# Two-block decoder kernel: 128 tokens of the expert layer gathered instead of 96, 384 dense columns instead of 416, weight splits and roundings moved between engines

## The chip, the cores and the metric

The kernel runs on one core of one Trainium2 chip. The metric is the device time in microseconds (us). Before the change three runs gave 3052.07, 3065.22 and 3062.26 us, median 3062.26. The execution that the hardware profiler took lasted 3056.66 us and has a span of 3054.9 us.

## The reference

512 tokens of width 1024 go through a first block (convolution and latent attention in parallel, then an expert layer called PEER) and a second block of two layers (short convolution, sparse attention, each with a gated feed-forward layer). The change is in the expert layer alone:

```
q = (xb @ wq).reshape(C, PEER_HEADS, 2, PEER_DK_HALF)
s = jnp.einsum('chpd,hpnd->chpn', q, keys)          # 8 heads, 2 halves, 128 keys
sv, si = lax.top_k(s, 16)
cand = sv[:, :, 0, :, None] + sv[:, :, 1, None, :]
top_s, sel = lax.top_k(cand.reshape(C, PEER_HEADS, 256), 16)
eidx = ...                                            # one of 16384 experts, 8 x 16 a token
g = jax.nn.softmax(top_s, axis=-1)
act = gelu(einsum('chkd,cd->chk', u_tab[eidx], xb))
out = einsum('chk,chkd->cd', g * act, v_tab[eidx])
```

Each token chooses 128 of the 16384 experts, each a row of 1024 numbers in the table `peer_u` and one in `peer_v`.

## The kernel before, in words

Activations lie transposed, features on partitions. Every product of fp32 numbers is done as three products of rounded high and low parts (`product`, L305 to L309). Weight tiles (128 x 1024, 512 KB) run through `Feed`, a ring with three slots: SyncE (SP) loads a tile when the tile three before it is split (L253), ScalarE (ACT) rounds it to the high part when TensorE (PE) is done with the tile three before it (L262), and the low part is subtracted (L272, the "split") by VectorE (DVE) in the expert layer and by GpSimd (POOL) elsewhere.

The expert layer (`peer`) treats most tokens densely. All 16384 experts are computed for the first 416 tokens: a **U phase** of 128 tiles, of 24 products each, gives activations that ACT passes through gelu (L1627) and SP stores to DRAM (L1422); then a **V phase** of 128 tiles multiplies them, weighted with gates, into the eight PSUM banks. The gates are zero but for the chosen experts. They are built in the U phase from one-hot vectors: `gate_block` (L1528) makes eight tokens' gates with 16 small products, ACT copies them (L1608), SP stores them. In the V phase SP loads them again, eight tiles' gates at once (`load_gates`, L1409, 1664 KB), along with each tile's activations (L1415).

The last 96 tokens are gathered: POOL fetches expert rows by indirect DMA (L1463) into four buffers; VectorE multiplies each with the token's row and adds up (`first`, L1707, a dot) for the first table, and adds it with its weight (`second_of`, L1861) for the second. 64 tokens lie on two partitions each and 32 on four, so 96 steps of 128 rows do for each table; a spread of small DMAs (SP, L1423 to L1430) puts ids and token rows there, and products with `fold` matrices add the copies together at the end (L1570).

Which experts a token chooses is found by VectorE in four **routes**, one for each 128 tokens (L1721 to L1838): top 16 of 128 scores by `max`, `max_index` and `match_replace`, the sums, the top 16 again, and the decoding of places by comparisons. The order of the routes is 3, 0, 1, 2, so that the gathered tokens come first. All orders are written out by hand: `START`, `score_tile`, `turn_tile` and `block_tile` say at which U tile TensorE computes scores, turns the results of a route (`turn`, which waits for VectorE) and does which gate block. A route lasts 15 tiles, and within it VectorE calls `weights()` at 15 places, each of which splits the next tile. In the gate-block stretches VectorE does for each tile a split, the one-hot vectors (`hots`), and one dot (`early`); after the last route two dots a tile until 76 are done. The other 20 dots and all 96 steps of the second table are done in the V phase, at most one a tile. There VectorE does for tile n, in this order: gates times activations (L1880), the gather step, the weight split, the rounding of the weighted activations (L401) and their low part (L404). TensorE waits for the last of these.

Engines execute their instructions in order, and a wait holds all behind it.

Of the kernel before, what the change touches and what calls it, by code (L numbers as in the profile page):

```python
# [35 lines left out]
F32 = mybir.dt.float32  # L36
# [7 lines left out]
P = 128  # L44
# [179 lines left out]
class Feed:  # L224
# [50 lines left out]

    def take(self, pe, n):
        pe.wait_ge(self.split, n + 1)
        return self.hi[:, n % self.SLOTS, :], self.lo[:, n % self.SLOTS, :]


class Part:
# [12 lines left out]
    def split_to(self, eng, m):  # L294
        self.feed.split_to(eng, self.first + m)

# [915 lines left out]
GROUPS = ((64, 448), (32, 416))  # L1212
STEPS = sum(n for n, first in GROUPS)
DTOK = SEQ - STEPS
ROWS = 4
ROUTE = (3, 0, 1, 2)
Q_WEIGHTS = 15
EARLY = 76


def peer(kit, io):
# [4 lines left out]
    with Stage(kit, "peer") as st:  # L1226
# [38 lines left out]
        groups, small = [], 44032  # L1265
        for g, (n, first) in enumerate(GROUPS):
            s0 = sum(m for m, _ in GROUPS[:g])
            groups.append(dict(n=n, first=first, s0=s0, rep=P // n,
                               mine=at(f"chosen_here{g}", small, [P, 2, n], U32),
                               fold=at(f"fold{g}", small + 8 * n, [P, n])))  # L1270
            small += 12 * n
        dots = at("dots", small, [P, STEPS])
        share = at("shares", small + 4 * STEPS, [P, STEPS])
        assert small + 8 * STEPS <= 46080 and 2 * DTOK * QUAD * 4 <= 26624
        group_of = [g for g in groups for _ in range(g["n"])]
# [7 lines left out]
        rows = nc.alloc_sbuf_tensor_at("peer_token_rows", [P, D], F32, offset=G_at)  # L1283
        chosen = nc.alloc_sbuf_tensor_at("peer_chosen", [P, 2, PH * TOPK], U32, offset=G_at + 4 * D)
        for g, x in enumerate(groups):
            x["acc"] = nc.alloc_sbuf_tensor_at(f"peer_gather_sum{g}", [P, D], F32, offset=shared + g * D * 4)
# [8 lines left out]
        groups[0]["row"] = nc.alloc_sbuf_tensor_at("peer_row_here0", [P, D], F32, offset=io["mixT_at"] + 12288)  # L1295
        for g, x in enumerate(groups[1:]):
            x["row"] = st.sb(f"row_here{g + 1}", [P, D])
# [34 lines left out]
        spread = st.sem("tokens_spread")  # L1332
# [33 lines left out]
        TURN = Q_WEIGHTS + 1  # L1366
        blocks, START, of_route = [], [], []
        for r, j in enumerate(ROUTE):
            START.append(Q_WEIGHTS * r + len(blocks))
            mine = list(range(j * P, min((j + 1) * P, DTOK), HB))  # L1370
            of_route.append(range(len(blocks), len(blocks) + len(mine)))
            blocks += mine
# [9 lines left out]
        scored_first = sum(c <= TURN and half == 0 for c, (r, half) in score_tile.items())  # L1382
        n_spread = 32 * sum(x["rep"] for x in groups)
# [7 lines left out]
        def second_step(n):  # L1391
            return n - SHARES - 1 if 0 <= n - SHARES - 1 < STEPS else None

        with nc.Block() as block:

            @block.sync
            def _(sp):
# [19 lines left out]
                for c in range(NK + 1):  # L1417
# [5 lines left out]
                    if c == TURN + 3:  # L1423
                        sp.wait_ge(experts_known, 2)
                        sp.wait_ge(rows_copied, 1)
                        for x in groups:
                            n, t0 = x["n"], x["first"] - (SEQ - P)
                            for e in range(x["rep"]):
                                sp.dma_start(x["mine"][e * n:(e + 1) * n, :, :],
# [1540 lines left out]
```

## Time and profile before

| | |
|---|---|
| median of 3 runs | 3062.26 us |
| profiled execution | 3056.66 us, span 3054.9 us |
| PE busy | 2918.0 us, 96% of the span |
| PE weight loads (PEld) | 2591.1 us, 85% |
| DVE busy | 1802.1 us, 59% |
| ACT busy | 996.8 us, 33% |
| POOL busy | 999.0 us, 33% |
| U phase | 376.8 to 1068.2 us |
| V phase | 1068.2 to 1652.0 us |
| mean granted TensorE clock | 0.956 |

Busy times of PE and PEld overlap. A granted clock of 1 is 2.4 GHz; the lower level is 1.2 GHz. Times of an event are counted from the start of the span.

### The profile page before, as it was taken

Reading aid. Unit: us, or ns where it says so; the run is one execution under the profiler, and the core shown is the slowest. Engines: PE = TensorE matmul, PEld = TensorE weight load, DVE = VectorE, ACT = ScalarE, POOL = GpSimd, SP = SyncE. Lnnn points to the kernel's source line nnn. Section 1 sums busy time; section 2 is a strip of 40 time slices with the busy share of each in tenths; the row PEclk is TensorE's granted clock in tenths of the full one; section 3 lists DMA queues with packets and bytes.
Section 4 is the critical chain, followed back from the end, with each engine's and each line's share of the span. In section 5 each row is a group of like instructions: output and inputs, shape, how many; then the busy total and the mean of one; then the engine's idle time right before and its main releaser. Section 6 shows DMA issues by size and latency. Waiting matters only on the chain. (4 is left out here: it accounts for less than half of the span.)

```text
span 3054.9 us, 39382 instructions
## 1 busy us (share of the span) xinstructions
PE 2918.0 (96%) x15042; PEld 2591.1 (85%) x15042; DVE 1802.1 (59%) x3227; ACT 996.8 (33%) x1582; POOL 999.0 (33%) x611
## 2 busy tenths in 40 slices
PE   8887999999999799999999999999999899999998
PEld 7554799999999799999998787888788898778886
DVE  6785777888887677887884843331143455333311
ACT  4345233443434222222223223222223456332212
POOL 3201500111112432433332544444432344454442
PEclk9767999999999899999999999999999789999999
DMA  3101256786959988999983232233331000223332
GB/s 130 34 1 42 95 145 206 225 277 200 296 179 308 385 294 304 329 324 329 331 305 113 90 104 83 97 97 102 98 130 31 4 1 15 76 83 97 97 103 70
DMA packets 195745, 475.83 MB, mean 156 GB/s; under 512 B 17205, under 2 KB 104117, under 8 KB 193253
## 3 DMA queue, kind: packets, MB, share of 16 engines
q1 hardware_dynamic: 167764, 370.54, 37.0%
q0 software_dynamic: 27648, 100.68, 9.5%
q8 instruction: 120, 1.97, 0.3%
q10 hardware_dynamic: 144, 2.10, 0.2%
q14 instruction: 69, 0.56, 0.0%
HBM read 415.47 MB, written 56.62 MB: 155 GB/s over the span
## 5 line engine op out<-in xcount | busy, mean ns | idle before, releaser
L262 ACT ACTIVATE w_hi<-w 128x1024 fp32r<-128x1024 f32 (+2 forms) x485 | 506.6, 1046 | 1236.3 <-DVE ffn_gates L2119 324.4
L272 POOL TENSOR_TENSOR w_lo<-w,w_hi 128x1024 fp32r<-128x1024 f32 (+2 forms) x229 | 542.4, 2379 | 693.6 <-ACT w_hi L262 693.6
L272 DVE TENSOR_TENSOR w_lo<-w,w_hi 128x1024 fp32r<-128x1024 f32 x256 | 313.5, 1225 | 190.7 <-ACT w_hi L262 158.5
L307 PE MATMUL peer_psum<-xn_hi,w_hi 128*128 128x416 f32 x1024 | 369.0, 360 | 16.2 <-ACT peer_act_out L1627 16.2
L308 PE MATMUL peer_psum<-xn_lo,w_hi 128*128 128x416 f32 x1024 | 363.2, 355 | 0.0
L309 PE MATMUL peer_psum<-xn_hi,w_lo 128*128 128x416 f32 x1024 | 362.7, 354 | 0.0
L307 PE MATMUL peer_psum<-peer_w_hi,w_hi 128*128 128x416 f32 x1024 | 359.8, 351 | 2.1 <-DVE peer_w_lo L404 1.4
L308 PE MATMUL peer_psum<-peer_w_lo,w_hi 128*128 128x416 f32 x1024 | 358.9, 350 | 0.0
L309 PE MATMUL peer_psum<-peer_w_hi,w_lo 128*128 128x416 f32 x1024 | 358.9, 350 | 0.0
L1463 POOL DMA_INDIRECT peer_gathered<-in_peer_u,peer_chosen_here x96 | 141.5, 1474 | 623.0 <-DVEq L1710 496.0
L307 PE MATMUL ffn_psum<-ffn_hn_hi,w_hi 128*128 128x512 f32 x704 | 275.8, 392 | 10.4 <-DVE ffn_hn_lo L617 6.6
L308 PE MATMUL ffn_psum<-ffn_hn_lo,w_hi 128*128 128x512 f32 x704 | 275.2, 391 | 0.0
L309 PE MATMUL ffn_psum<-ffn_hn_hi,w_lo 128*128 128x512 f32 x704 | 275.2, 391 | 0.0
L1463 POOL DMA_INDIRECT peer_gathered<-in_peer_v,peer_chosen_here x96 | 168.0, 1750 | 281.9 <-DVEq L1865 269.9
L307 PEld LDWEIGHTS peer_psum<-xn_hi,w_hi 128*128 128x128 f32 x1024 | 195.8, 191 | 19.6 <-issue 17.6
L308 PEld LDWEIGHTS peer_psum<-xn_lo,w_hi 128*128 128x128 f32 x1024 | 195.8, 191 | 1.3
L309 PEld LDWEIGHTS peer_psum<-xn_hi,w_lo 128*128 128x128 f32 x1024 | 195.2, 191 | 1.4
L307 PEld LDWEIGHTS peer_psum<-peer_w_hi,w_hi 128*128 128x128 f32 x1024 | 192.4, 188 | 4.2 <-issue 2.1
L308 PEld LDWEIGHTS peer_psum<-peer_w_lo,w_hi 128*128 128x128 f32 x1024 | 192.4, 188 | 1.1
L309 PEld LDWEIGHTS peer_psum<-peer_w_hi,w_lo 128*128 128x128 f32 x1024 | 192.4, 188 | 1.0
L1627 ACT ACTIVATE peer_act_out<-peer_psum 128x416 f32<-128x416 f32 x128 | 66.3, 518 | 340.1 <-PE peer_psum L309 280.3
L307 PEld LDWEIGHTS ffn_psum<-ffn_hn_hi,w_hi 128*128 128x128 f32 x704 | 133.0, 189 | 41.5 <-issue 7.4
(417 smaller groups left out, 5724.5 us busy)
## 6 DMA issues: line engine op xcount, KB each, us to landing
w<-in_peer_uT SPq DMA_DIRECT2D x128, 512.0 KB
w<-in_peer_v SPq DMA_DIRECT2D x128, 512.0 KB
w<-in_f_w_gu SPq DMA_DIRECT2D x88, 512.0 KB
peer_act<-peer_act_out SPq DMA_DIRECT2D x128, 208.0 KB
peer_gate<-peer_gates_out SPq DMA_DIRECT2D x26, 1024.0 KB, 8.1
peer_gates<-peer_gate SPq DMA_DIRECT2D x16, 1664.0 KB, 9.6
peer_act_in<-peer_act SPq DMA_DIRECT2D x128, 208.0 KB
w<-in_f_w_down SPq DMA_DIRECT2D x32, 512.0 KB
```

What stands on the lines that cost most here:

```text
L262: act.activation(self.hi[:, x, 0:c], self.buf[:, x, 0:c], ACT.Copy).then_inc(self.rounded, 1)
L272: eng.tensor_tensor(self.lo[:, x, 0:c], self.buf[:, x, 0:c], self.hi[:, x, 0:c].bitcast(F32), ALU.subtract).then_inc(self.split, 1)
L307: pe.matmul(out, w[0], x[0], start=start, stop=False)
L308: pe.matmul(out, w[0], x[1], start=False, stop=False)
L309: return pe.matmul(out, w[1], x[0], start=False, stop=stop)
L1463: pool.indirect_dma_start(G[:, s % ROWS, :], None, table, bass.IndirectOffsetOnAxis(here[:, 0, at0:at0 + 1], 0))\
L1627: act.activation(Ao[:, c % AS, 0:DTOK], ps[:, c % 2, 0:DTOK], ACT.Gelu).then_inc(gelued, 1)
```

## The change

The gathered tokens are the first 128, one on each partition: 128 steps for each table, no spread, no fold matrices, and the token rows stay where ACT wrote them. The dense columns are tokens 128 to 511, 384 of them; gate blocks are 48. Routes run in the order 0 to 3, with 13, 16, 16 and 16 tiles. In a route POOL splits the weight tiles and, from route 1 on, fetches one row set behind each split; VectorE calls `beside` at the places where it split before, which does one dot (every fourth time two), none in route 0. After the routes one dot a tile is done until 112. In the V phase ACT rounds the weighted activations, behind its rounding of the next weight tile; VectorE does 16 dots and then spreads the 128 steps of the second table over 107 tiles. The first load of gates goes out eight tiles before the end of the U phase, the second in the V phase.

```diff
+    def split_one(self, eng, n):
+        c, x = self.tiles[n].shape[1], n % self.SLOTS
+        eng.wait_ge(self.split, n)
+        eng.wait_ge(self.rounded, n + 1)
+        eng.tensor_tensor(self.lo[:, x, 0:c], self.buf[:, x, 0:c], self.hi[:, x, 0:c].bitcast(F32),
+                          ALU.subtract).then_inc(self.split, 1)
...
-GROUPS = ((64, 448), (32, 416))
-STEPS = sum(n for n, first in GROUPS)
-DTOK = SEQ - STEPS
+GT = 128
+STEPS = PH * TOPK
+DTOK = SEQ - GT
 ROWS = 4
-ROUTE = (3, 0, 1, 2)
-Q_WEIGHTS = 15
-EARLY = 76
+Q_WEIGHTS = (13, 16, 16, 16)
+EARLY = 112
+PACE = 99
...
-            turn_tile[START[r] + TURN] = r
+            turn_tile[START[r] + Q_WEIGHTS[r] + 1] = r
             for i, b in enumerate(of_route[r]):
-                block_tile[START[r] + TURN + 1 + i] = b
+                block_tile[START[r] + Q_WEIGHTS[r] + 3 + i] = b
...
+        def dot_beside(b):
+            return b not in of_route[0] and b % PACE != PACE - 1
...
-        def second_step(n):
-            return n - SHARES - 1 if 0 <= n - SHARES - 1 < STEPS else None
+        def second_steps(n):
+            return [s for s in range(STEPS) if SHARES + 1 + s * (NK - 2 - SHARES) // STEPS == n]
...
-                    if c == TURN + 3:
-                        sp.wait_ge(experts_known, 2)
-                        sp.wait_ge(rows_copied, 1)
-                        for x in groups:
...
-                    if c == NK - 6:
+                    if c == NK - 8:
                         for i in range(2):
                             sp.wait_ge(g_stored[i], 16 * len(range(i, n_slices, 2)))
-                        for q in range(2):
-                            load_gates(q)
+                        load_gates(0)
+                    if c == NK - 6:
                         for n in range(AS):
                             sp.wait_ge(a_stored[n], 16)
                             load_act(n)
...
                     load_act(n)
+                    if n == AS + 1:
+                        load_gates(1)
...
-                pool.wait_ge(spread, n_spread)
-                for s in range(2 * STEPS):
+                fetched_to = 0
+                for r in range(ST):
+                    for n in range(Q_WEIGHTS[r]):
+                        lin.ring.split_one(pool, U0 + START[r] + n + 2)
+                        if r == 1 and n == 0:
+                            pool.wait_ge(experts_known, 2)
+                            for s in range(ROWS):
+                                fetch(s, t["peer_u"])
+                            fetched_to = ROWS
+                        if r:
+                            fetch(fetched_to, t["peer_u"])
+                            fetched_to += 1
+                    for b in of_route[r]:
+                        if dot_beside(b):
+                            fetch(fetched_to, t["peer_u"])
+                            fetched_to += 1
+                for s in range(fetched_to, 2 * STEPS):
                     fetch(s, t["peer_u"] if s < STEPS else t["peer_v"])
...
-                                     xn.pair(slice(None), k, slice(0, DTOK)), k == 0, k == DT - 1)
+                                     xn.pair(slice(None), k, slice(GT, SEQ)), k == 0, k == DT - 1)
...
-                            for x in groups:
-                                mm = pe.matmul(ps[:, d, x["first"]:x["first"] + x["n"]], x["acc"][:, p], x["fold"][:, :],
-                                               start=True, stop=True)
+                            mm = pe.matmul(ps[:, d, 0:GT], acc[0:GT, p], kit.ident[0:GT, 0:GT], start=True, stop=True)
...
-                lin.ring.round_to(act, V0 + SHARES)
-                act.wait_ge(dotted, 1)
-                act.activation(dots[:, :], dots[:, :], ACT.Gelu).then_inc(dots_gelued, 1)
+                for n in range(NK):
+                    lin.ring.round_to(act, V0 + n + 2)
+                    if n == SHARES - 1:
+                        act.wait_ge(dotted, 1)
+                        act.activation(dots[0:GT, :], dots[0:GT, :], ACT.Gelu).then_inc(dots_gelued, 1)
+                    if n >= WS:
+                        lin.ring.done_by(act, V0 + n - WS + 1)
+                    act.wait_ge(weighed, n + 1)
+                    act.activation(Ws.hi[:, n % WS, 0:DTOK], Wf[:, n % 2, 0:DTOK], ACT.Copy).then_inc(w_hi, 1)
...
                 def weights():
 
                     ahead[0] += 1
-                    lin.ring.split_to(dve, U0 + min(ahead[0] + 2, NK))
+                    lin.ring.split_one(dve, U0 + ahead[0] + 1)
...
+                def beside(r):
+
+                    placed[r] += 1
+                    for _ in range((2 if placed[r] % 4 == 0 else 1) if r else 0):
+                        early()
...
-                    if n >= WS:
-                        lin.ring.done_by(dve, V0 + n - WS + 1)
                     lin.ring.split_to(dve, V0 + n + 1)
-                    dve.wait_ge(weighed, n + 1)
-                    Ws.write_hi(dve, (slice(None), n % WS, slice(0, DTOK)), x).then_inc(w_hi, 1)
                     dve.wait_ge(w_hi, n + 1)
                     Ws.write_lo(dve, (slice(None), n % WS, slice(0, DTOK)), x).then_inc(w_lo, 1)
```

## Rows read from the trace of the kernel before

**Rows 1.** Stretches, all engines: length, busy PE, PEld, DVE, ACT, POOL, clock, DMA share, GB/s

```profile
376.80:1068.20 691.40, 665.26 (x4076) 645.70 (x4076) 552.25 (x1394) 262.65 (x390) 115.60 (x82) 0.98 0.77 247
1068.20:1652.00 583.80, 582.12 (x3104) 578.22 (x3104) 469.09 (x646) 136.04 (x130) 193.87 (x110) 1.00 0.85 302
```

**Rows 2.** Waits in the U phase: who waited for whom, us, times, longest

```profile
PE peer_psum L307 <- ACT peer_act_out L1627: 16.2, 3, 11.6
```

**Rows 3.** Timeline: start us, us, what; PE at 264 columns, ACT at 416, POOL at 512

```profile
97.83 0.28 PE L309 MATMUL front_psum<-xn_hi,w_lo 128*128 128x264 f32 x1
...
100.38 0.29 PE L309 MATMUL front_psum<-xn_hi,w_lo 128*128 128x264 f32 x1
...
1404.74 1.06 ACT L262 ACTIVATE w_hi<-w 128x1024 fp32r<-128x1024 f32 x1 [3.46 <-PE peer_psum L309]
...
1440.90 1.06 ACT L262 ACTIVATE w_hi<-w 128x1024 fp32r<-128x1024 f32 x1 [3.46 <-PE peer_psum L309]
...
1819.50 2.40 POOL L272 TENSOR_TENSOR w_lo<-w,w_hi 128x1024 fp32r<-128x1024 f32 x1 [3.04 <-ACT w_hi L262]
```

**Rows 4.** Timeline of weight loads in the U phase, one gate block

```profile
475.63 0.90 PEld L1528 LDWEIGHTS peer_psum<-peer_first_hot,peer_second_hot 128*128 128x128 f16 x16 [0.18 <-issue]
```

**Rows 5.** Timeline of DVE in the V phase, one tile

```profile
1401.35 0.58 DVE L1880 SCALAR_TENSOR_TENSOR peer_w<-peer_gates,peer_act_in 128x416 f32<-128x416 f32 x1
1401.85 1.28 DVE L1861 SCALAR_TENSOR_TENSOR peer_gather_sum<-peer_gathered,peer_shares,peer_gather_sum 128x1024 f32<-128x1024 f32 x1
1403.34 1.23 DVE L272 TENSOR_TENSOR w_lo<-w,w_hi 128x1024 fp32r<-128x1024 f32 x1 [0.21 <-DVE peer_gather_sum L1861]
1404.49 0.37 DVE L401 CAST peer_w_hi<-peer_w 128x416 fp32r<-128x416 f32 x1
1404.89 0.59 DVE L404 TENSOR_TENSOR peer_w_lo<-peer_w,peer_w_hi 128x416 fp32r<-128x416 f32 x1
```

**Rows 6.** Timeline of SP's loads and ACT's roundings in the V phase, two pairs

```profile
1088.28 0.43 SPq L253 DMA_DIRECT2D w<-in_peer_v  x1
...
1093.47 1.06 ACT L262 ACTIVATE w_hi<-w 128x1024 fp32r<-128x1024 f32 x1 [3.46 <-DMA w<-in_peer_v]
...
1402.80 1.51 SPq L253 DMA_DIRECT2D w<-in_peer_v  x1
...
1414.02 1.06 ACT L262 ACTIVATE w_hi<-w 128x1024 fp32r<-128x1024 f32 x1 [8.22 <-DMA w<-in_peer_v]
```

**Rows 7.** Stretch in the U phase: length, PE busy, clock, DMA share, GB/s

```profile
540.00:580.00 40.00, 38.07 (x228) 0.96 0.57 177
```

**Rows 8.** Stretches with gate stores (PE alone) and in the V phase (columns as rows 1)

```profile
740.00:780.00 40.00, 39.86 (x300) 1.00 0.93 300
...
1300.00:1600.00 300.00, 300.00 (x1595) 298.20 (x1594) 248.03 (x327) 70.93 (x67) 111.36 (x63) 1.00 0.90 324
```

**Rows 9.** Timeline of ACT at the end of the U phase

```profile
1059.76 0.52 ACT L1627 ACTIVATE peer_act_out<-peer_psum 128x416 f32<-128x416 f32 x1 [18.22 <-DMA peer_act<-peer_act_out]
```

**Rows 10.** One route: DVE busy in it, and its splits alone

```profile
481.90:554.70 72.80, 59.71 (x234) 1.00 0.72 224
...
481.90:554.70 72.80, 18.37 (x15) 1.00 0.72 224
```

**Rows 11.** Timeline of DVE in the U phase, a dot and what follows

```profile
643.09 1.22 DVE L1707 SCALAR_TENSOR_TENSOR peer_gathered<-peer_gathered,peer_row_here 128x1024 f32<-128x1024 f32 x1
...
644.46 1.23 DVE L272 TENSOR_TENSOR w_lo<-w,w_hi 128x1024 fp32r<-128x1024 f32 x1
```

**Rows 12.** Timeline of POOL and DVE in the next stage; L2014 by itself

```profile
1791.33 2.59 POOL L272 TENSOR_TENSOR w_lo<-w,w_hi 128x1024 fp32r<-128x1024 f32 x1 [0.75 <-ACT w_hi L262]
...
1791.70 2.77 DVE L2014 SCALAR_TENSOR_TENSOR hT<-hT,gains,short_gf_rs 128x512 f32<-128x512 f32 x1
...
L2014 DVE SCALAR_TENSOR_TENSOR hT<-hT,gains,short_gf_rs x8: 751/1760/2770, 1702.2 to 1791.7; 128x512 f32<-128x512 f32 x8
```

**Rows 13.** Groups in the U phase: busy us, mean ns, idle before

```profile
L1463 POOL DMA_INDIRECT peer_gathered<-in_peer_u,peer_chosen_here x82 | 115.6, 1410 | 578.8 <-DVEq L1710 451.8 <-DMA peer_row_here<-peer_token_rows 124.9 <-issue 2.1
```

More of the change, by code:

```diff
@@ L1263, in peer @@
         A = at("act_in", 46080, [P, AS, SEQ])
[L1265 to L1275, printed above, removed]
+        mine = at("chosen", 44032, [P, 2, STEPS], U32)
+        dots = at("dots", 45056, [P, STEPS])
+        share = at("shares", 45568, [P, STEPS])
+        assert 2 * DTOK * QUAD * 4 <= 26624
         shared = nc.sbuf_base
@@ L1282, in peer @@
         G = nc.alloc_sbuf_tensor_at("peer_gathered", [P, ROWS, D], F32, offset=G_at)
[L1283 to L1286, printed above, removed]
+        acc = nc.alloc_sbuf_tensor_at("peer_gather_sum", [P, D], F32, offset=shared)
         an_bufs = (at("an_sq", 4096, [P, 2, SEQ]), at("an_rs", 8192, [P, SEQ]), io["attn_sum"])
@@ L1365, in peer @@
         PER = HB // 4
-        TURN = Q_WEIGHTS + 1
         blocks, START, of_route = [], [], []
[L1368 to L1372, printed above, removed]
+        for j in range(ST):
+            START.append(sum(Q_WEIGHTS[:j]) + len(blocks))
+            here = list(range(max(j * P, GT), (j + 1) * P, HB))
+            of_route.append(range(len(blocks), len(blocks) + len(here)))
+            blocks += here
         n_blocks, per_slice = len(blocks), QB // HB
@@ L1726, in _ @@
                         if i == 7:
-                            weights()
+                            beside(r)
                     own.wait()
-                    weights()
+                    beside(r)
                     for i in range(NS):
@@ L1733, in _ @@
                         if i % 6 == 5:
-                            weights()
+                            beside(r)
                     own.wait()
@@ L1739, in _ @@
                         if i == 7:
-                            weights()
+                            beside(r)
                     own.wait()
-                    weights()
+                    beside(r)
                     for i in range(NS):
@@ L1762, in _ @@
                     own.wait()
-                    weights()
+                    beside(r)
                     for h in range(PH):
@@ L1767, in _ @@
                     own.wait()
-                    weights()
+                    beside(r)
                     for h in range(PH):
@@ L1773, in _ @@
                         own.step(dve.max_index(sel[:, h, 8:16], tops[:, h, 8:16], left[:, h, :]))
[L1774 removed]
+                    beside(r)
                     own.step(dve.tensor_copy(tot[:, :], tops[:, :, 0]))
@@ L1797, in _ @@
                                                abf[:, 2:4, :].rearrange("p i (h k) -> p i h k", h=PH), ALU.add))
-                    weights()
+                    beside(r)
                     for i in range(2):
@@ L1803, in _ @@
                     own.wait()
-                    weights()
+                    beside(r)
                     for i in range(2):
@@ L1812, in _ @@
                     own.link(dve.tensor_tensor(three[:, 0:2, :], eq[:, :, 0, :], eq[:, :, 1, :], ALU.add))
-                    weights()
+                    beside(r)
                     dve.wait_ge(exped, r + 1)
@@ L1868, in _ @@
                     weights()
-                    for _ in range(2):
-                        early()
+                    early()
                 assert dotted_to[0] == EARLY
+                if EARLY == STEPS:
+                    own.wait()
+                    dve.nop().then_inc(dotted, 1)
                 for n in range(NK):
```

88 lines of the change are left out of this document (36 added, 52 removed).

## The prediction

> **What bounds the kernel now.** I read the table of stretches first: the expert part is two stretches. In the first (the U phase, 376.8 to 1068.2 us) TensorE multiplies the 128 weight tiles of `peer_uT`; in the second (the V phase, 1068.2 to 1652.0) those of `peer_v`. TensorE is busy 665.3 of 691.4 us and 582.1 of 583.8 [rows 1]. All other stretches run code that the change leaves alone, so the sum is made over these two. Next the waits of TensorE: in the U phase the largest is 16.2 us, behind ScalarE's copy of the results [rows 2]; in the V phase there is next to none. So a saving on TensorE counts in full unless something else becomes late, and a new lateness counts in full too.
>
> Then I ask whether TensorE is paced by its weight loads, since the loads' busy share reaches 99% in the V phase. The starts of consecutive products say no. With 264 columns, 21 products take 2.55 us, 121 ns each, with the same 128-column loads. With 416, eight tiles of 24 products take 36.16 us (from one tensor-released rounding to the one eight tiles later), 188.3 ns each. With 512 a tile lasts 2.40 + 3.04 us, 226.7 ns each [rows 3]. The load records overlap; the columns set the pace. Between the first two widths a column costs 0.44 ns, between the last two 0.40.
>
> **Part 1, 416 to 384 columns.** 32 columns fewer at 0.40 to 0.44 ns are 12.8 to 14.1 ns; I take 14, so a product takes 174.3 ns and a tile 4.18 us where it took 4.52. The 2 x 3072 products of the two phases would save 43 us each, 86 us together, if their operands came in time. The gate blocks fall from 52 to 48; one holds TensorE for about 0.9 us [rows 4]: 4 us saved. The eight pairs of fold products at the end become eight products: about 2 us.
>
> **Part 2, the V phase: a wait that moves.** Before, VectorE did all for tile n by itself: gate times activation (start to start 0.50 us), one gather step (1.49), weight split (1.15), rounding (0.40), low part (0.59): 4.1 us [rows 5]. After it drops the rounding, does 128 gather steps over 107 tiles (1.20 x 1.49 = 1.78 us) and comes to 4.0 us, still under 4.18. The rounding (some 0.5 us, as ScalarE's copy of 416 columns, 0.52 [rows 9]) goes to ScalarE, which has room: its weight rounding is 1.06 us. But ScalarE issues its work in order: it rounds weight tile n+1 and only then the activations of tile n. So tile n cannot start on TensorE until the weights of n+1 have landed, and 1.06 + 0.5 + VectorE's low part and handovers, 2.3 us in all, have passed. Before, tile n+1's weights were needed one tile later.
>
> How late do they land? The load issued at 1402.80, right behind a load of gates, is rounded at 1414.02 (loads and roundings paired by counting), 11.2 us later, where TensorE would have allowed it at 1404.74 + 4.52 = 1409.26; a load with nothing in front takes 1093.47 - 1088.28 = 5.2 us [rows 6]. TensorE did not feel it, since it took that tile at 1418.3. (The same recurs every 36 us, at each load of gates.) After: the load of tile m goes out when VectorE has weighed tile m-2, and VectorE is now itself tied to ScalarE, so it goes out some 3.6 us after TensorE starts tile m-4 (2.3 for the low part of m-3, 0.5 to weigh, 0.8 for SP's issues in front of it). It has to have landed 2.3 us before TensorE starts tile m-1. That leaves 3 x 4.18 - 2.3 - 3.6 = 6.6 us. An ordinary load (5.2 us) fits. One behind the gates (1536 KB where it was 1664, so about 10.3 us) is 3.7 us late, and TensorE stands. The load two tiles later goes out late in turn, behind a queue not yet drained: nothing to 2.4 us more, I take 1.2. A stop of about 2 us also lowers the clock: the stretch with such a stop shows a granted clock of 0.96 over 40 us [rows 7], 3.2 us at the lower of two levels, so 1.5 us more. A period of eight tiles is then 33.4 + 3.7 + 1.2 + 1.5 = 39.8 us, where it was 36.2. There are 14 such periods and 16 tiles without: 14 x 39.8 + 16 x 4.18 = 624 us. At the start of V, VectorE can no longer run ahead of TensorE (ScalarE must first finish the U phase), and tile 3 waits for activations that are fetched only after the last of them is stored: 6 us, bounds 1 and 12. Sum 630 less 2 for the fold: **+44 us** against 583.8. Bounds: 540 us (no stop, -44), and 655 (+71).
>
> The bytes are the check. Per tile 0.52 MB of weights, 0.20 of activations, 0.20 of gates and 1.2 x 0.52 gathered are 1.55 MB; at 39.8 us for eight that is 311 GB/s. The DMA engines gave 324 at a share of 0.90 in the V phase and 300 at 0.93 while gates are stored [rows 8]. At 4.18 us a tile they would have to give 370, so the full column gain is unlikely there even without the moved wait.
>
> **Part 3, the U phase.** While gates are stored each tile moves 0.52 + 0.20 + 0.52 + 0.52 = 1.77 MB; at 300 / 0.93 = 322 GB/s that takes 5.5 us, about what such a tile took before (4.52 + 0.96). So I count no column gain in the 48 block tiles, and 80 x 24 x 14 ns = 27 us in the others. (Bounds 27 and 43.)
>
> The end of U: two loads of gates were issued together six tiles before the end, and two gather steps ran per tile; a result copy then waited 18.2 us for its buffer [rows 9], most of the 16.2 us of [rows 2]. Now one load of gates goes out earlier and one gather step runs per tile: I take 14 us saved with the clock, bounds 5 and 19.
>
> The routes. One route costs VectorE 59.7 us of which 18.4 are splits: 41.3, say 42 with handovers [rows 10]. Splits go to POOL; in routes 1 to 3 come 18 dot products (first-table steps) at 1.37 us each [rows 11]: 66.7 us. The time that TensorE gives: from when VectorE is through with the last gate block to the next turn are one block tile and fifteen plain ones, with VectorE's lead some 70 us; for route 1, 67. That would just fit. But POOL's split and a VectorE instruction with two SBUF inputs get in each other's way: at 1791.33 POOL starts a split of 2.59 us, VectorE starts at 1791.70 an instruction that takes 0.75 us at its shortest, and it takes 2.77, to just after the split's end [rows 12]. In a route POOL splits 2.4 of every 4.18 us, so a dot meets a split in 57 of 100 cases and waits half of it: 0.69 us, 18 times 12.4, and some 2 for the other two-input instructions. That makes 81 us: TensorE stands at the turn 14 us in route 1 and 11 in route 2. In route 3 the dots are just as far as the fetches, so each waits for a split (ends 3.9 us after the tile starts), an indirect fetch (1.4 us [rows 13]), its landing and itself. As many bytes took a plain load 5.2 us from issue to use; for the landing behind the 1.4 I take 3, and the dot is 1.4: dot 15 ends 9.8 us into its tile, 11 us of routing and two dots are left, and the turn is due 8.4 us after that tile's start: 13 us late. Together 38 us and three drops of the clock at 1.5: **43 us**. Bounds: 5 (waits fall into the slack) and 65: in route 1, POOL's fetch waits for the dot and its next split for the fetch, 1.4 + 2.4 + 1.4 = 5.2 us a round where TensorE wants 4.18.
>
> The Trainium skill, "SBUF — State Buffer", section "SBUF: two separate sides", has the rule behind it: the port pair that VectorE and GpSimd share is an exclusive lock, and the later one waits for the whole instruction. The trace agrees (2.77 us for 0.75). By the rule a part of the splits' relief comes back as waiting, 43 us in the sum; without it the routes would cost only route 3's 13.
>
> The spread of chosen experts and rows over groups (12 small DMAs behind SP's wait) goes: 1 us at most, off the path.
>
> U phase: -27 - 4 - 14 + 43 = -2 us. **Sum:** 3056.7 - 2 + 44 = 3099 us for a profiled execution; the median of the three runs shown (3062.3) lies 5.6 above the profiled one, so 3104.
>
> **Rivals.** A: the column gain arrives. V runs at 4.18 us a tile with few stops (550 us) and the routes fit (10 us late): U -27 - 4 - 14 + 10 = -35, V -34, so 2993. For it: VectorE has slack in both phases, and a share of 0.90 leaves the DMA engines a tenth. Against: the 11.2 us behind every load of gates, 14 of them.
> B: DMA alone sets V. The 188 MB that V moves at 321 GB/s take 586 us, the moved wait costs nothing beyond that, routes 25 us late: U -20, V +2, so 3044. For it: shares near 0.9 already. Against: before, loads could land five to six us late unseen.
> C: the round of dot, fetch and split that hands the lock back and forth (5.2 against 4.18 us) holds in all three routes: 48 rounds at 1 us, with clock drops 65 us, and V at its upper bound 655: 3062 + 20 + 71, 3153. It decides from the point where POOL's split of a tile ends after TensorE asks for it.
> D: the change moves work but VectorE gains nothing, since every split taken off it is waited for in the lock. It is the upper half of C's U phase, in C's chance.
>
> **Chances.** Forecast 0.48 (own range 3070 to 3145), A 0.22, B 0.2, C 0.1. A measurement tells a change from none at about 0.5%, 15 us: 3047 to 3078. Faster: A and half of B and a little, 0.33. Same: the rest of B and the forecast's low end, 0.15. Slower 0.52. Range 2990 to 3155.
>
> **What would show it.** Right: TensorE's waits in V appear once per eight tiles, released by `peer_w_lo` and preceded by ScalarE's rounding waiting for the DMA of `peer_v`; the granted clock in V falls under 1; products start 174 ns apart; dots in routes last over 2 us; the turn of each route is waited for; the wait at the end of U is gone. Wrong: ScalarE's roundings in V are released by TensorE only (then A), products stay 188 ns apart (no column gain), or VectorE's dots keep 1.22 us beside POOL's splits.

## The result and the profile after

| | before | after |
|---|---|---|
| median | 3059.5 us (4 runs, 3052.1 to 3065.2) | 3149.7 us (4 runs, 3144.5 to 3152.2) |
| profiled execution | 3056.7 us | 3152.0 us |
| U phase, first product to first product of V | 687.9 us | 718.4 us |
| V phase, first to last product | 583.2 us | 645.0 us |

The change made the kernel slower by 3.0% (ratio 1.030, 95% interval 1.027 to 1.033), 90 us where the forecast had 42. The direction holds, and so does the wide range (2990 to 3155); the forecast's own range, 3070 to 3145, was missed by 5 us, and the size is more than twice the forecast. Between the profiled executions 95.3 us were lost: 30.5 in U, 61.8 in V, 3.0 elsewhere.

The stretches below are cut at the first product of a phase, so that kernels compare: before, then after. Columns: stretch, length, busy PE, granted clock, DMA share, GB/s.

```profile
380.50:1068.40 687.90, 661.59 (x4061) 0.98 0.77 247
1068.40:1651.60 583.20, 581.72 (x3100) 1.00 0.85 302
```

```profile
383.60:1102.00 718.40, 625.64 (x3998) 0.94 0.78 253
1102.00:1747.00 645.00, 569.64 (x3088) 0.93 0.83 292
```

TensorE is busy for 48 us less and idle for 140 us more, and the granted clock is lower. The waits of TensorE after, in U (four rows) and in V (the last), as [rows 2]:

```profile
PE peer_psum L1514 <- DVE peer_three L1835: 37.5, 3, 15.0
PE peer_psum L319 <- ACT peer_act_out L1631: 23.8, 4, 13.6
PE peer_psum L1534 <- ACT peer_gates_out L1612: 22.7, 10, 5.5
PE peer_psum L319 <- POOL w_lo L280: 7.0, 7, 2.2
...
PE peer_psum L319 <- DVE peer_w_lo L416: 76.7, 19, 6.8
```

**V.** The waits come once per eight tiles. Two of TensorE's starts after such a wait, 40.72 us apart:

```profile
1449.17 0.66 PE L319 MATMUL peer_psum<-peer_w_hi,w_hi 128*128 128x384 f32 x1 [3.91 <-DVE peer_w_lo L416]
...
1489.89 0.66 PE L319 MATMUL peer_psum<-peer_w_hi,w_hi 128*128 128x384 f32 x1 [4.58 <-DVE peer_w_lo L416]
```

ScalarE shows why. Between stops it rounds a weight tile every 4.16 us, released by TensorE: that is the new tile, 24 products of 173 ns. Then it stands 9.13 us at the DMA, and the activations are rounded only behind it (compare [rows 5, 6]):

```profile
1472.92 1.06 ACT L262 ACTIVATE w_hi<-w 128x1024 fp32r<-128x1024 f32 x1 [2.69 <-PE peer_psum L321]
1473.88 0.51 ACT L1640 ACTIVATE peer_w_hi<-peer_w 128x384 fp32r<-128x384 f32 x1
1477.08 1.06 ACT L262 ACTIVATE w_hi<-w 128x1024 fp32r<-128x1024 f32 x1 [2.69 <-PE peer_psum L321]
1478.05 0.51 ACT L1640 ACTIVATE peer_w_hi<-peer_w 128x384 fp32r<-128x384 f32 x1
1487.68 1.06 ACT L262 ACTIVATE w_hi<-w 128x1024 fp32r<-128x1024 f32 x1 [9.13 <-DMA w<-in_peer_v]
1488.64 0.51 ACT L1640 ACTIVATE peer_w_hi<-peer_w 128x384 fp32r<-128x384 f32 x1
```

The load that it waits for stood behind a load of gates; by count it is the one issued at 1476.32, and 11.4 us passed until it was rounded:

```profile
1475.84 0.43 SPq L1409 DMA_DIRECT2D peer_gates<-peer_gate  x1
1476.32 0.43 SPq L253 DMA_DIRECT2D w<-in_peer_v  x1
```

The chain reads: load lands 1487.7, weights rounded, activations rounded until 1489.15, VectorE's low part 1489.18, product 1489.89. The weights that were late belong to a later tile; this tile's own had been in place since the rounding before.

**U.** Each turn of a route is waited for, and ScalarE stands before it too: its Exp of route 3 waits 16.45 us for VectorE, results queue up behind it, and TensorE waits 13.61 us for a result bank. At the turn itself it waits 15.01 more. ScalarE's row first, then TensorE's:

```profile
898.09 0.31 ACT L1623 ACTIVATE peer_tops<-peer_tops 128x128 f32<-128x128 f32 x1 [16.45 <-DVE peer_tops L1795]
...
900.35 0.66 PE L319 MATMUL peer_psum<-xn_hi,w_hi 128*128 128x384 f32 x1 [13.61 <-ACT peer_act_out L1631]
...
926.21 0.90 PE L1514 MATMUL peer_psum<-ident,peer_three 128*128 128x128 f32 x3 [15.01 <-DVE peer_three L1835]
```

VectorE is late for two reasons. The first is that it works beside POOL's splits. In each pair below VectorE's instruction ends after POOL's split by no more than the time that it takes alone (1.10 and 0.29 us): a dot (1.22 us beside nothing) takes 2.77, and a decoding step of the route, whose shortest is 0.42, takes 3.10:

```profile
691.98 2.42 POOL L280 TENSOR_TENSOR w_lo<-w,w_hi 128x1024 fp32r<-128x1024 f32 x1
...
692.73 2.77 DVE L1716 SCALAR_TENSOR_TENSOR peer_gathered<-peer_gathered,peer_token_rows 128x1024 f32<-128x1024 f32 x1
...
713.44 2.40 POOL L280 TENSOR_TENSOR w_lo<-w,w_hi 128x1024 fp32r<-128x1024 f32 x1
...
713.03 3.10 DVE L1810 TENSOR_TENSOR peer_abf<-peer_abf,peer_second 128x256 f32<-128x256 f32 x1
```

The Trainium skill, "SBUF — State Buffer", section "SBUF: two separate sides", says that of a VectorE instruction with two SBUF inputs and a GpSimd one that reads SBUF, the one that starts first has the shared ports for its whole length and the other is blocked. The first pair agrees. In the second VectorE's row starts 0.41 us before the split's and waits even so; it shows the waiting, but not that the later one waits.

The second reason is that VectorE waits for gathered rows to land: 22.9 us in U, 15.9 of them in route 3. The longest of these waits stands between ScalarE's Exp (898.09) and the turn (926.21). By count, the row is the one of the fetch below, which stands on POOL behind the split above it:

```profile
901.30 2.38 POOL L280 TENSOR_TENSOR w_lo<-w,w_hi 128x1024 fp32r<-128x1024 f32 x1 [13.35 <-ACT w_hi L262]
903.82 0.95 POOL L1454 DMA_INDIRECT peer_gathered<-in_peer_u,peer_chosen  x1
...
909.35 1.23 DVE L1716 SCALAR_TENSOR_TENSOR peer_gathered<-peer_gathered,peer_token_rows 128x1024 f32<-128x1024 f32 x1 [9.02 <-DMA peer_gathered<-in_peer_u,peer_chosen]
```

The split had waited 13.35 us for ScalarE's rounding, and ScalarE was held by its Exp: VectorE's lateness comes back to VectorE.

The granted clock falls with the stops. Three stretches of U and V that hold some, to be read beside [rows 7]:

```profile
700.00:740.00 40.00, 20.73 (x94) 0.74 0.52 166
900.00:940.00 40.00, 24.64 (x131) 0.76 0.54 177
1440.00:1480.00 40.00, 35.95 (x191) 0.91 0.87 303
```

### The profile page after: what moved, and what is told of

Its sections match the earlier page's. It is cut to its first block and busy times, and to the rows that moved or that the text cites. A ratio compares the mean times of both kernels' runs of the same rounds, so it can differ in the third digit from the quotient of the medians.

```text
span 3150.2 us, 39539 instructions
## 1 busy us (share of the span) xinstructions
PE 2878.6 (91%) x14962; PEld 2549.3 (81%) x14962; DVE 1816.0 (58%) x3113; ACT 1040.8 (33%) x1702; POOL 1249.8 (40%) x736
## 5 line engine op out<-in xcount | busy, mean ns | idle before, releaser
L319 PE MATMUL peer_psum<-peer_w_hi,w_hi 128*128 128x384 f32 x1024 | 358.6, 350 | 77.1 <-DVE peer_w_lo L416 76.7
L319 PE MATMUL peer_psum<-xn_hi,w_hi 128*128 128x384 f32 x1024 | 357.4, 349 | 30.8 <-ACT peer_act_out L1631 23.8
L1454 POOL DMA_INDIRECT peer_gathered<-in_peer_v,peer_chosen x128 | 221.7, 1732 | 343.0 <-DVEq L1876 319.0
L320 PE MATMUL peer_psum<-peer_w_lo,w_hi 128*128 128x384 f32 x1024 | 354.7, 346 | 0.0
L321 PE MATMUL peer_psum<-peer_w_hi,w_lo 128*128 128x384 f32 x1024 | 353.7, 345 | 0.0
L320 PE MATMUL peer_psum<-xn_lo,w_hi 128*128 128x384 f32 x1024 | 349.8, 342 | 0.0
L321 PE MATMUL peer_psum<-xn_hi,w_lo 128*128 128x384 f32 x1024 | 349.7, 342 | 0.0
L1454 POOL DMA_INDIRECT peer_gathered<-in_peer_u,peer_chosen x128 | 188.0, 1468 | 339.8 <-DVEq L1719 325.4
L1716 DVE SCALAR_TENSOR_TENSOR peer_gathered<-peer_gathered,peer_token_rows 128x1024 f32<-128x1024 f32 x128 | 185.8, 1451 | 24.7 <-DMA peer_gathered<-in_peer_u,peer_chosen 22.9
L280 POOL TENSOR_TENSOR w_lo<-w,w_hi 128x1024 fp32r<-128x1024 f32 x61 | 150.2, 2462 | 101.2 <-ACT w_hi L262 100.5
L1631 ACT ACTIVATE peer_act_out<-peer_psum 128x384 f32<-128x384 f32 x128 | 62.9, 491 | 335.0 <-PE peer_psum L321 219.0
```

The costliest lines, as they stand in the source:

```text
L280: eng.tensor_tensor(self.lo[:, x, 0:c], self.buf[:, x, 0:c], self.hi[:, x, 0:c].bitcast(F32), ALU.subtract).then_inc(self.split, 1)
L319: pe.matmul(out, w[0], x[0], start=start, stop=False)
L320: pe.matmul(out, w[0], x[1], start=False, stop=False)
L321: return pe.matmul(out, w[1], x[0], start=False, stop=stop)
L1454: pool.indirect_dma_start(G[0:GT, s % ROWS, :], None, table, bass.IndirectOffsetOnAxis(mine[0:GT, 0, s % STEPS:s % STEPS + 1], 0))\
L1631: act.activation(Ao[:, c % AS, 0:DTOK], ps[:, c % 2, 0:DTOK], ACT.Gelu).then_inc(gelued, 1)
```

## The experiments

All were timed beside the kernel before; ratios are to it. "U" and "V" are the lengths of the two phases as above (before 687.9 and 583.2, after 718.4 and 645.0).

### The order on ScalarE in V

**e1_order.** The kernel after, with one call moved:

```diff
                 for n in range(NK):
-                    lin.ring.round_to(act, V0 + n + 2)
                     ...
                     act.wait_ge(weighed, n + 1)
                     act.activation(Ws.hi[...], Wf[...], ACT.Copy).then_inc(w_hi, 1)
+                    lin.ring.round_to(act, V0 + n + 2)
```

> The changed kernel with one edit: in the V phase ScalarE rounds the weighted activations of tile n before it rounds weight tile n+1. Theory (the moved wait): TensorE's stops in V (76.7 us in 19 waits, behind a granted clock of 0.93) come from the activations of n standing in line behind the landing of weights n+1. Then most stops go, V falls from 645 us to 560 to 585, and the time to 3065 to 3090. Rival (DMA alone sets V): the 188 MB at the 321 GB/s of before need 586 us and the higher demand only lengthens the queue; V stays at 600 or more, and the time falls by less than 45 us.

Measured 3061.0 us, ratio 1.001 (1.000 to 1.003), 4 us below the expected range. V is 563.7 us, 81 less than after; U is unchanged (719.8). TensorE's waits in V fall from 76.7 to 23.9:

```profile
1104.00:1667.70 563.70, 541.58 (x3088) 0.99 0.92 335
```

```profile
PE peer_psum L319 <- DVE peer_w_lo L416: 23.9, 17, 5.8
```

**e5_before_act.** The opposite test: only that edit, in the kernel before, with its 416 columns, its routes and its dots.

```diff
-                lin.ring.round_to(act, V0 + SHARES)
+                for n in range(NK):
+                    lin.ring.round_to(act, V0 + n + 2)
+                    ...
+                    act.wait_ge(weighed, n + 1)
+                    act.activation(Ws.hi[...], Wf[...], ACT.Copy).then_inc(w_hi, 1)
...
-                    Ws.write_hi(dve, (slice(None), n % WS, slice(0, DTOK)), x).then_inc(w_hi, 1)
```

> The kernel before with one part of the change alone: ScalarE rounds the weighted activations in V, behind its rounding of the next weight tile. 416 columns, 96 gathered, routes as before. Theory (the moved wait): one stop of about 2 to 3 us at each of 14 loads of gates, with 1.5 to 2 us of lower clock behind each, V from 583 to 625 to 645 us, the time 40 to 60 us above before. Rival (V is slow in the changed kernel for its higher DMA demand): the demand is that of before, VectorE is relieved, and the time is within 10 us of before.

Measured 3145.9 us, ratio 1.027 (1.025 to 1.030). The one edit alone costs as much as the whole change: 86 us against the median in the table, 89 against the kernel before as timed beside it, where 40 to 60 were expected. V is 666.5 us: 83 more. 57.2 are waits; for the rest, TensorE is busy 29 us longer for the same products, at a lower granted clock:

```profile
1074.30:1740.80 666.50, 611.12 (x3102) 0.95 0.78 264
```

```profile
PE peer_psum L307 <- DVE peer_w_lo L404: 57.2, 16, 5.1
```

So a stop of 3.6 us on average (57.2 / 16) cost 5.2 us (83.3 / 16).

**e2_gate_pieces.** The kernel after, with each load of gates cut in four pieces, each piece behind a different tile's activations.

```diff
-                    if n % QUAD == QUAD - 2 and 2 <= n // QUAD + 1 < NK // QUAD:
-                        load_gates(n // QUAD + 1)
+                    if QUAD - 6 <= n % QUAD < QUAD - 2 and 2 <= n // QUAD + 1 < NK // QUAD:
+                        load_gates(n // QUAD + 1, n % QUAD - 2)
```

> The changed kernel with each load of gates cut into four of 384 KB that go out behind four successive tiles. Same bytes. Theory (the moved wait with late weights): the load of weights behind a piece is 1 to 1.5 us later than an ordinary one, 6 to 7 us, at the 6.6 us that the order allows; the stops shrink to under 25 us in all, V to 555 to 590 us, the time to 3070 to 3095. Rival (bytes set V): the same bytes take the same time, within 20 us of 3150.

Measured 3114.6 us, ratio 1.019 (1.015 to 1.023), V 608.7 us; 3070 to 3095 and 555 to 590 were expected. The stops were to shrink to under 25 us and did not. Behind the one at the start of V (5.6 us) none is longer than 3.4, but there are 52 in all, 54.3 us: many loads are a little late, and by after's order the lateness is felt. The load of gates decides where the stops gather, the order how much of a late load TensorE feels. Together (**a1_order_pieces**: both edits) they leave next to nothing:

> The changed kernel with both edits in the V phase: activations rounded before the next weights, and the gates loaded in four pieces. Theory (the stops in V come from late weights; 24 us of them and 7 us of low clock are left with the first edit): V falls from 563 to 540 to 550 us, the time is 3040 to 3052, a little under the kernel before. Rival (what is left in V is a bound of VectorE or of the bytes): V stays within 6 us of 563, the time at 3055 to 3065.

Measured 3055.6 us, ratio 0.999 (0.997 to 1.000), V 545.1 us at a clock of 1.00 and 346 GB/s. Six waits are left, 9.5 us, of which 5.8 at the start of V. That is the column gain of V, 38 of the 43 us that 3072 products of 14 ns would give. V fell as expected; the total missed its range by 4 us. It was counted from e1, whose profiled execution was 9 us above its own median, and U is 722.3 here. The gates moved and cut in the kernel before (**b1_before_loads**) brought nothing:

> The kernel before with only the loads of gates moved: the first eight tiles before the end of U, the second in V, the others cut in four. Theory (the 15.9 us stop at the end of U was two loads of gates in one go): the stop goes, V is unchanged since nothing was late for TensorE there, 3038 to 3048. Rival (the stop comes from two dots a tile and the stores): within 5 us of before.

Measured 3054.8 us, ratio 1.000 (0.998 to 1.001): U 682.7, V 590.1. Of the 16.2 us stop at the end of U 8.4 stay, and V begins with a new wait of 6.7 us. After has no stop there; besides its earlier load it does one dot a tile at that place where b1 does two. The versions a3 and a5 below have after's earlier load and two dots a tile, and there a stop of 5.9 and 5.2 us stands 17 us before V: the pace of the dots counts, and the load alone is not enough.

### The routes in U

Four kernels make a square: who splits in the routes, and whether VectorE does dots there. **e4_vector_splits** is the kernel after with the splits of the routes back on VectorE (POOL only fetches). **e6_no_route_dots** and **e7_before_routes** have no dots in routes, up to two a tile after the last route, the other 57 in V, and e1's order in V; POOL splits in e6 and VectorE in e7. All three in short:

```diff
-                        lin.ring.split_one(pool, U0 + START[r] + n + 2)     # e4, e7
...
                     placed[r] += 1
+                    if placed[r] <= Q_WEIGHTS[r]:                           # e4, e7
+                        lin.ring.split_one(dve, U0 + START[r] + placed[r] + 1)
-                    for _ in range((2 if placed[r] % 4 == 0 else 1) if r else 0):   # e6, e7
-                        early()
```

> The changed kernel with the weight splits of the four routes back on VectorE, at the same places; the dots stay in the routes and POOL only fetches. Theory (the lock takes the relief back): VectorE loses 16 x 1.15 = 18 us a route to the splits and gains as much or more by not waiting for POOL's; the waits at the turns stay within 10 us in all of the 37.5 before, and the time within 15 us of 3150. Rival (the splits on POOL are a real relief, and the routes are just too long): each route gets 12 to 18 us longer, TensorE waits 35 to 50 us more at the turns, and the time is near 3190.

> The kernel after with the V phase in the better order (ScalarE rounds activations first) and with no dots in the routes: POOL still splits there, VectorE does only the routing; after the last route two dots are done in two of three tiles, 71 before V, and V has the other 57, so VectorE is overloaded in V (two gather steps in most tiles, 0.5 + 2 x 1.49 + 1.15 + 0.59 = 5.2 us a tile for about 66 tiles): only the U phase is to be read. Theory (dots beside POOL's splits, and one-off instructions blocked by them, made VectorE late): a route then costs about 41 us plus some 10 of blocked instructions, under the 67 that TensorE gives, so TensorE waits at no turn and not for Exp; what stays is the gates' way out (23 to 30 us). U 680 to 690. Rival (splits on POOL alone make the routes late through the lock): turn waits of 5 us or more a route stay, U over 700. Whole kernel 3060 to 3120 because of V.

> As the last, but VectorE splits in the routes, so that the routes are those of the kernel before (59.7 us of VectorE each), with 384 dense columns, 48 gate blocks and a dot in each gate-block tile. Only the U phase is to be read. If the column gain arrives in the tiles without gate stores: 687.9 - 27 - 4 - 14 = 643 us. If VectorE's own way of calling the splits (waits of up to 3 us each, since the pieces of a route are longer than a tile of 4.18 us) eats it: TensorE waits 20 to 40 us for w_lo in the routes and U is 670 to 690. In e4 that wait was 38.1 us with 18 dots a route; if it falls under 10 here, the dots made it. Waits for the gates' way out (27.5 in e4) should stay, which takes U to about 665.

Measured: e4 3135.2 us, ratio 1.025 (1.022 to 1.028); e6 3032.4, 0.993 (0.990 to 0.995); e7 3037.3, 0.993 (0.990 to 0.995). Their U phases, in the order e4, e6, e7:

```profile
382.70:1088.50 705.80, 633.88 (x3997) 0.96 0.82 257
```

```profile
379.60:1026.90 647.30, 613.86 (x3997) 0.97 0.77 247
```

```profile
383.60:1034.50 650.90, 614.02 (x3998) 0.97 0.77 246
```

| U phase, us | VectorE splits | POOL splits |
|---|---|---|
| no dots in routes | 650.9 | 647.3 |
| 17 or so dots in routes 1 to 3 (51 in all) | 705.8 | 718.4 |

Dots cost 55 us with VectorE's splits and 71 with POOL's. Moving the splits to POOL costs 12.6 us where VectorE does dots. Where it does none it saves 3.6, which is no more than U varies between kernels with the same U code (718.2 to 722.3 in after, e1, e2 and a1): no gain is shown. e4 fell into its time range, but not by its theory: the waits at the turns were to stay and fell from 37.5 to 4.1 us, and 38.1 us of waits for `w_lo`, the low part of the weights, stand in their place. e7's U is 8 us above its first case (643) and under the others; its wait for `w_lo` is gone, so in e4 it was the dots that made it. e6 missed what I expected of it by over 30 us: I had thought that U would keep a good part of the loss. VectorE is still held beside POOL's splits in e6: the routing instructions (all but dots, splits and the gates' one-hot vectors) take VectorE 246 us there and 196 in e7, so 50 of the 75 us that 61 splits of 1.23 us gave free came back as longer instructions; but a route without dots has slack and absorbs it. After compared with e4 closes the sum where there are dots: VectorE's splits take 75 us less, its dots 30 more, the routing 30 more, the gates' one-hot vectors 4 more, and it waits 23 us for rows to land where e4 never does. 87 us came back for 75, and U is 12.6 longer. One group, e6 and then e7; behind the bar: busy us, mean ns:

```profile
L1827 DVE TENSOR_TENSOR peer_eq<-peer_eq 128x2048 f16<-128x2048 f16 (+2 forms) x12 | 23.9, 1994 | 0.4
```

```profile
L1828 DVE TENSOR_TENSOR peer_eq<-peer_eq 128x2048 f16<-128x2048 f16 (+2 forms) x12 | 9.4, 781 | 0.4
```

**e3_exp_later.** The kernel after, with ScalarE's Exp one tile before the turn and not four.

```diff
-                    if c + 4 in turn_tile:
+                    if c + 1 in turn_tile:
```

> The changed kernel; ScalarE's exponential of each route's scores, for which it waits on VectorE, stands one tile before the turn and not four. In the changed kernel this wait holds ScalarE 31 us and TensorE 22 us in routes 2 and 3, besides the waits at the turns. Theory (VectorE is late, wherever it is waited for): TensorE runs on and then waits longer at the turn, 37.5 us become 50 to 60, and the time stays within 8 us of 3150. Rival (the wait of ScalarE is a loss of its own): 15 to 25 us faster.

Measured 3141.5 us, ratio 1.028 (1.026 to 1.030), U 715.2. The wait for result banks falls from 23.8 to 4.5 us and the wait at the turn rises from 37.5 to 57.0: the sum, 61 us, is VectorE's lateness, wherever TensorE meets it.

### Versions that should be faster

**a2_balanced** is a1 with routes of 17 tiles, of which VectorE splits the last four, and 10 dots a route.

> As a1, and the U phase with less on VectorE while POOL splits: routes of 17 tiles, 13 split by POOL and the last 4 by VectorE (so that its two-input steps at the end of a route meet no split), 10 dots a route where there were 18, up to 2 dots a tile after the routes, 101 before V. Theory (dots and decoding steps meet POOL's splits, some 20 us a route are waiting): VectorE needs 42 + 14 + 5 + 8 = 69 us for a route of 71, the turns are waited for less than 12 us in all, U falls from 717 to 650 to 670, V gets 0 to 8 us longer, the time 2985 to 3010. Rival (U is bound by the bytes of the block stretches and by the fetches): U stays above 690 and the time above 3020.

Measured 3013.4 us, ratio 0.986 (0.983 to 0.989): U 680.4, V 547.4. No turn is waited for, as expected, but U misses its range (650 to 670) by 10 us: POOL's splits, result banks and the gates' copies are still waited for (11.3, 10.7 and 30.4 us). **a3_dots_to_v** is a1 with no dots in routes; 50 dots go into the first 30 tiles of V. **a4_few_route_dots** has four dots a route:

```diff
-                        if r:
+                        if r and n < ROUTE_DOTS:      # a3: 0, a4: 4, a5: n in (2, 5, 8, 11)
                             fetch(fetched_to, t["peer_u"])
...
-                    for _ in range((2 if placed[r] % 4 == 0 else 1) if r else 0):
-                        early()
+                    if r and placed[r] in (2, 5, 8, 11):      # a4, a5
+                        early()
```

> The kernel after with ScalarE's activations first and the gates in four pieces (a1), no dots in the routes (e6), two dots a tile after the last route until 78, the other 50 over 30 tiles of V and the 128 steps of the second table over the remaining 93. U as in e6, 647 us. In V VectorE needs 0.5 + 1.15 + 0.59 + 1.39 x 1.49, about 4.3 us a tile against TensorE's 4.18: V 555 to 565, whole kernel 2985 to 3000 if VectorE's mean sets it. Rival 1: slack lets single tiles pass and V is as in a1 (545), 2975 to 2985. Rival 2: every tile with two gather steps is waited for, as in e6 (43.6 us in 50 tiles): V 600, whole 3035.

> As a3_dots_to_v, with four dots in each of routes 1 to 3 (behind the 2nd, 5th, 8th and 11th split), so 38 dots in V over 24 tiles. With 0 dots a route U was 647 us, with 18 it was 720, with 10 (in a2, routes of 17 tiles) 680. If a route has slack (some 52 us of VectorE's time against 67 to 70 that TensorE gives) four dots of 1.7 us fit: U stays 647 to 650, V falls by up to 12 x 1.49 = 18 us against a3, whole 5 to 18 us under a3. If the price is per dot from the first on, (720 - 647) / 54 = 1.35 us a dot: U 663, whole kernel equal to a3 or slower.

a3 took 3004.0 us, ratio 0.983 (0.981 to 0.985): U 659.3 where 647 was expected, V 562.3. a4 took 3061.3, ratio 1.001 (1.000 to 1.002), with U at 715.0, which neither of my two cases had. TensorE waits 48.1 us in U for POOL's splits. POOL issues in order, and the fetch of a row waits for the dot that frees its buffer; I had put four fetches behind the first four splits of a route, so the next split stood behind a fetch that waited 11.10 us (POOL's queue):

```profile
475.68 2.40 POOL L280 TENSOR_TENSOR w_lo<-w,w_hi 128x1024 fp32r<-128x1024 f32 x1
489.17 0.95 POOL L1459 DMA_INDIRECT peer_gathered<-in_peer_u,peer_chosen  x1 [11.10 <-DVEq L1724]
490.14 7.26 POOL L280 TENSOR_TENSOR w_lo<-w,w_hi 128x1024 fp32r<-128x1024 f32 x3
```

**a5_fetch_in_step** puts each fetch behind the split at which its dot is called, and changes nothing else.

> a4_few_route_dots with one thing mended: there POOL's four fetches of a route stood behind its first four splits, so a fetch waited up to 11 us for the dot that frees its row, and the next split stood behind the fetch (TensorE waited 48.1 us for POOL's splits). Here each fetch stands behind the split after which its dot is called. If a few dots fit into a route (slack of 15 us, four dots of 1.7 us), U is 647 to 657 and V as in a4 (558): 2990 to 3002 in all, 0 to 10 us under a3. If the price is per dot, 1.35 us each and more, U is 663 or more and the whole 3005 to 3015.

Measured 2999.3 us, ratio 0.982 (0.979 to 0.984): U 653.6, V 558.9. So the 61 us between a4 and a5 are the price of the order of fetches on POOL, and four dots a route are nearly free. a3 and a5 can't be told apart by their intervals; both beat the kernel before, as timed beside them, by 53 to 60 us.

```profile
382.90:1036.50 653.60, 614.63 (x3998) 0.97 0.81 261
1036.50:1595.40 558.90, 541.67 (x3087) 0.99 0.95 357
```

## Why the prediction was half the size of the loss

**Right.** The pace: 173 ns a product, 4.16 us a tile (174.3 and 4.18 forecast). The moved wait in V: it recurs every eight tiles, behind the load of gates, preceded by ScalarE's wait for the DMA, and falls to a third when the order is turned (e1, 76.7 to 23.9 us). Its size too, in part by luck: 3.7 us behind the gates and 1.2 at a later load were forecast for each period; the 13 periods from 1165.94 to 1693.39 hold 62.9 us of it, 4.8 each, but 4.7 of that is the first stop and 0.1 the second. The load behind the gates took 11.4 us where I had put 10.3. The stop at the start of V was 5.6 us (6). The turns: 11.9, 10.6 and 15.0 us (14, 11, 13). The stop at the end of U is gone. So the structure of the forecast stood. What failed are three terms of its sum: the clock in V, the routes in U, and the gain in U.

**The clock in V: 1.5 us a period forecast.** The period measures (1693.39 - 1165.94) / 13 = 40.57 us (39.8 forecast). Less 8 x 4.16 = 33.28 and 4.8 of waits, 2.5 us are left for the lower clock. Over the whole of V (645.0 - 532.5 - 76.7) 36 us went that way where 21 were forecast, and TensorE's busy time agrees (569.6 us, 37 over 532.5). I had taken the price of one stop from [rows 7], a stretch with only 0.96; a stretch of V with a stop shows 0.91. This makes most of V's 61.8 where 44 were forecast. e5 says the same from the other side.

**The routes in U: 43 us forecast.** e7, with VectorE's splits and no dots in the routes as in the kernel before, and the rest of U nearly as in after (its dots behind the routes come faster), has U at 650.9: the routes as changed cost 718.4 - 650.9 = 67.5 us. The part at the turns was right (37.5 against 38). What I left out is ScalarE: its Exp waits for the same VectorE four tiles before the turn, and what stands behind it on ScalarE stops TensorE for another 23.8 us; e3 shows that it is the same lateness. Together VectorE is 8.7 + 10.6 = 19 us late in route 2 and 13.6 + 15.0 = 29 in route 3, and not 11 and 13. Its dots didn't make the difference: they take 1.78, 1.70 and 1.70 us on average in the three routes, 0.5 over their 1.22 where 0.69 was forecast. But to all other instructions of a route I gave 2 us of waiting, and they take 227 us in after's four routes against 196 in e7's, 7.7 a route; 3.10 where 0.42 was due is one row of them. In route 3 the mechanism was the forecast's, dots behind a split, a fetch and its landing, but the split there had waited for ScalarE's Exp as well, which the forecast didn't have. I also let the Exp's stop go unpriced in the clock: the two stretches of U above have 0.74 and 0.76, where I had given 1.5 us a route, the price of a clock of 0.96 over 40 us.

**The other terms of U: 45 us of gain forecast** (27 + 4 + 14). e7 shows 687.9 - 650.9 = 37. TensorE stands 20 to 31 us for the gates' copies in all versions with after's 384 columns, and 2.7 in the kernel before. I had left out the column gain in the 48 block tiles (16 us), which is to say that it would be lost; in e7 24 us more than before go there, and the 8 beyond the 16 are the size of the shortfall.

The sum: V 18 us more than forecast, routes 24 more, the gain in U 8 less, 3 us elsewhere: 53, the difference between 95 and 42.

**The rivals.** A (columns arrive, 2993) is near what a version without the moved waits gives: a5, with four dots a route and the gates in pieces, reaches 2999. B's bound by the DMA engines at 321 GB/s isn't one: a1 draws 346, a3 366. C's price was nearly the one measured (3153), but by luck, since the way was another: neither a round of 5.2 us nor V at its upper end. Its mechanism, a fetch that waits for a dot while the split waits for the fetch, did show, in a4; in after POOL's splits cost TensorE just 7.0 us. D (all relief comes back) holds where dots run beside the splits, by the square above, but 23 of the 87 us that came back are waits for rows and not for the lock.

The 55 us that dots cost under VectorE's own splits are in two places: TensorE waits 38.1 us for `w_lo` in e4 and never in e7, and it is busy 20 us longer at a lower clock. Its wait at the turns is 4.1 us in both.

**Open.** How much of VectorE's lateness at each turn comes from instructions held beside the splits and how much from rows that land late was not separated by a run.

## What to carry to other kernels

Before work is given to an idle engine, write down what that engine waits for just ahead of it: the new place inherits each of those waits, and here one line of order was worth 81 to 83 us of V, 86 to 89 of the whole, while the work moved was 0.5 us a tile. Follow a lateness to every engine that waits for the late one, not to the last of them alone, and give each stop the clock's price from a stretch that has such stops. In a queue that also fetches (POOL here), a fetch into a ring belongs behind the last work that can be done before its buffer comes free.

## What the hardware showed that I had not expected

- Moving 61 splits from VectorE (1.23 us each) to POOL (2.4 us each) changed U by 3.6 us, within its spread, where VectorE had no dots. It isn't the long instructions alone that are held beside the splits: the routes' short ones, 0.2 to 1.2 us each by themselves, took 31 us more in after than in e7, and 50 more in e6.
- A recurrent stop of 3.6 us costs 5.2 with the clock (e5), one of 4.8 costs 7.3 (after): some 1.5 times itself.
- The DMA engines gave 366 GB/s at a share of 0.96 in a3's V phase, where the kernel before drew 302 to 324.
